# An input projection in two panels of seven products, with the row transposes moved between modulation steps

## The chip, the cores and the metric

The kernel runs on one core of a Trainium2 chip. The metric is the device time of one execution in microseconds (us). The work is float32 throughout.

## The reference, cut to what matters

The program computes three layers of a network. Only the start of the first one is touched: 512 latent rows `x` and 256 context rows `ctx` of width 1024 are normalised, modulated and multiplied by `w_in` (1024 x 2080).

```python
mod_x = (silu(c) @ w_ada + b_ada)            # 6 vectors of 1024: sh1, sc1, g1, sh2, sc2, g2
mod_c = silu(c_ctx) @ w_ada + b_ada
p_x = modulate(rmsnorm(h, norm_mix_w), sh1, sc1) @ w_in
p_c = modulate(rmsnorm(hc, norm_mix_w), csh1, csc1) @ w_in
# columns of p: q 256, k 256, v 512, g 512, r_f 16, r_b 16, pool_in 512
gk = log_sigmoid(r @ w_gk + b_gk) / 16       # for both directions
```

Of the context rows only k, v and r are needed. Behind this stand a gated linear attention with pooling (the mixer), an output product, and a layer of 32 experts which adds rows into a scratch array in memory that has to be zero beforehand.

## The kernel before, in words

The first block of the program works in stages, and the order on every engine is written out by hand; engines wait for each other by semaphores. At the end of the block all engines meet before the next block (the mixer) begins.

Weights pass through `ring`, a ring of tiles of 1 MB. In this block it has 8 slots, 0 to 7 (`MIX_SLOTS`). SP issues the loads in the order of the list `stream.tiles`; the load of tile n goes into slot n mod 8 and waits until the tile that held the slot is released (`stream.load`, line 188). The counter of releases is in order: `release` puts one on a matmul, and `owe` leaves it to be paid by the next `settle` or `release`. The list begins with tiles 0 to 7, eight blocks of `w_ada` (shift and scale of the first norm), then four tiles of `w_in` for q, k and v, and then, twice, two tiles of `w_in` and eight of `w_ada`. A tile of `w_in` is cut into rows of 2 KB per partition, a tile of `w_ada` into rows of 4 KB, in two issues.

In order of time TensorE does this:

- Three transposes bring the small vectors into columns (line 856). They wait for all constants `cst` (952 KB) and the vectors.
- Eight modulation steps (`vector_step`, line 543): four matmuls with 32 stationary columns each, side by side in the array, on one tile of `w_ada`. Their result is copied by VectorE (line 797), turned (line 571) and becomes `mod1` and `amix`.
- 48 transposes of x and ctx (lines 867 and 871) into `hT`, channels on partitions. ScalarE (x) and VectorE (ctx) move them out of PSUM and apply scale and shift on the way.
- q and k of x and k of the context (`project`, line 402), then r (line 891), v with the four `gates` between (line 902), g with eight further modulation steps between, and the pool input with the last eight.

VectorE and ScalarE empty PSUM, and between that turn r into the decays: `zb`, a log-sigmoid in three passes, four scans (line 835), `dve_shift`, `act_power`, `dve_scale`. GpSimd loads x and ctx, and when `mod_ready` is 3 it issues one DMA that fills the 20 MB of `y_scratch` with zeros (line 733); it waits for that DMA inside the block.

`Panel` and `Sums` are used by later layers. They compute a product of 512 x 1024 by 1024 x 1024 from four blocks of the weights and four of the rows with seven products of half the size in every direction instead of eight (Winograd's form). VectorE makes the sums of the weights t3, t2, t4, t1 in place, one after another, and the sums of the rows s1 to s4. Three pairs of the seven products add up in the same PSUM banks. A product is 16 matmuls of 256 columns (`channel_product`, line 459) or 8 of 512 (`token_product`, line 447).

## Time and profile before

| | us |
|---|---|
| median of 3 runs | 2180.89 |
| range of the 3 runs | 2178.28 to 2184.44 |
| the profiled execution | 2184.99 |
| its span on the core | 2182.8 |
| first matmul of q and k | 47.97 |
| first transpose of the mixer | 208.89 |

The span begins with the first instruction on the core; the 2.2 us between it and the time of the execution lie around it. Times inside are counted from the start of the span. An engine's busy time is the time in which it had an instruction in work; DMA queue q1 is the one that SP and ScalarE issue to in hardware, q0 is GpSimd's.

### The profile page before, as it was taken

How to read it: one execution, taken by the hardware profiler on the slowest of the kernel's cores; microseconds unless marked ns; L12 is line 12 of the kernel's file. 1: busy time of each engine (PE TensorE's matmuls, PEld its weight loads, DVE VectorE, ACT ScalarE, POOL GpSimd, SP SyncE). 2: the span in 40 equal slices, each digit the busy share in tenths (PEclk: the TensorE clock that was granted, in tenths of full speed). 3: DMA queues.
4: the chain of work that ended last, by engine and by line, in shares of the span. 5: the costliest groups of instructions: out<-in, count | busy, mean ns of one | idle time of the engine just before them, and what ended most of it. 6: DMA issues, size and time to landing. Idle time of an engine off the chain costs nothing.

```text
span 2182.8 us, 35887 instructions
## 1 busy us (share of the span) xinstructions
PE 2114.5 (97%) x14889; PEld 1141.3 (52%) x14889; DVE 950.8 (44%) x1640; ACT 491.0 (22%) x876; POOL 216.2 (10%) x266
## 2 busy tenths in 40 slices
PE   5999899999999999999999999899999999999998
PEld 2434545344444544444354443588584448777643
DVE  1041625833223223322322344754577625597742
ACT  2030312111101101110110110311126102666560
POOL 1000001121121122112112232200000000000000
PEclk9999999999999999999999999999999999999999
DMA  9957137999999999999999999723121032212200
GB/s 378 351 193 258 61 119 315 422 415 400 409 410 407 414 413 409 416 413 415 411 416 413 410 420 419 292 78 109 39 101 54 1 105 79 97 58 97 97 20 38
DMA packets 111830, 565.88 MB, mean 259 GB/s; under 512 B 16933, under 2 KB 29010, under 8 KB 77938
## 3 DMA queue, kind: packets, MB, share of 16 engines
q1 hardware_dynamic: 88950, 512.93, 58.4%
q0 software_dynamic: 19584, 49.84, 6.4%
q10 hardware_dynamic: 3228, 2.17, 0.3%
q8 instruction: 47, 0.77, 0.1%
q14 instruction: 21, 0.17, 0.0%
HBM read 545.21 MB, written 37.62 MB: 267 GB/s over the span
## 4 chain that ended last, share of the span: by engine, by line
PE 80%; DVE 3%; DMA 3%; issue 1%; ACT 1%; ACTq 0%; SPq 0%; DVEq 0%; POOLq 0%
PE ps L2309 30%; PE ps L459 11%; PE ps L2279 11%; PE ps L3848 5%; PE ps L3747 4%; PE ps L2287 4%; PE ps L447 3%; PE ps L1533 2%; PE ps L3727 2%; PE ps L3279 1%; DMA ring<-in_w_gu 1%; PE ps L3270 1%; DMA ring<-in_odd_w_in 1%; PE ps L2899 1%; PE ps L2943 1%
## 5 line engine op out<-in xcount | busy, mean ns | idle before, releaser
L2309 PE MATMUL ps<-ring,xeT 128*32 128x512 f32 x6144 | 684.5, 593 | 3.0 <-issue 1.7
L2309 PEld LDWEIGHTS ps<-ring,xeT 128*32 128x32 f32 x6144 | 259.9, 110 | 392.4 <-issue 335.5
L2279 PE MATMUL ps<-ring,mT 128*32 128x512 f32 x2048 | 322.3, 592 | 0.0
L2287 PE MATMUL ps<-ring,mT 128*32 128x256 f32 x2048 | 264.1, 379 | 0.0
L2048 DVE TENSOR_TENSOR mT<-ps,spread_bias 128x768 f32<-128x768 f32 x32 | 30.6, 957 | 462.5 <-PE ps L2309 462.4
L1986 ACT ACTIVATE mT<-mT 128x768 f32<-128x768 f32 x32 | 27.0, 845 | 867.0 <-DVE mT L2048 838.4
L2287 PEld LDWEIGHTS ps<-ring,mT 128*32 128x32 f32 x2048 | 118.3, 110 | 96.7 <-issue 66.2
L459 PE MATMUL ps<-hT_late,ring 128*128 128x256 f32 x704 | 155.5, 379 | 1.1 <-issue 1.1
L2279 PEld LDWEIGHTS ps<-ring,mT 128*32 128x32 f32 x2048 | 122.9, 110 | 52.8 <-issue 9.2
L459 PEld LDWEIGHTS ps<-hT_late,ring 128*128 128x128 f32 x704 | 133.4, 190 | 22.2 <-issue 4.1
L3848 PE MATMUL ps<-ring,mT 128*128 128x512 f32 x256 | 110.4, 592 | 0.0
L1808 POOL DMA_INDIRECT xe<-xn_scratch,idx x93 | 96.6, 1038 | 30.6 <-issue 28.7
L1819 ACT ACTIVATE xeT<-xturned,modx 128x96 f32<-128x96 f32 x248 | 91.8, 453 | 9.7 <-PE ps L2309 9.7
L2075 DVE STREAM_TRANSPOSE mT<-mT 128x768 f32<-128x768 f32 x31 | 30.3, 978 | 142.0 <-PE ps L2287 141.9
L3848 PEld LDWEIGHTS ps<-ring,mT 128*128 128x128 f32 x256 | 48.6, 190 | 60.8 <-issue 60.7
L1839 POOL TENSOR_TENSOR mark<-cst 128x1 f32<-128x1 f32 x57 | 11.9, 210 | 686.9 <-DVE ysb L2087 643.8
L402 PE MATMUL ps<-ring,hT 128*128 128x512 f32 x160 | 71.7, 598 | 0.0
L402 PE MATMUL ps<-hT,ring 128*128 128x512 f32 (+1 forms) x160 | 64.5, 556 | 2.2 <-DVE vtok L840 1.5
L1533 PE MATMUL ps<-ring,mixT 128*128 128x512 f32 x128 | 56.7, 596 | 2.4 <-DMA ring<-in_w_out 1.2
L1922 POOL DMA_INDIRECT y_scratch<-ysb,y_idx x54 | 55.6, 1029 | 23.1 <-issue 23.1
L459 PE MATMUL ps<-mT,ring 128*128 128x256 f32 x256 | 56.6, 379 | 0.0
L3747 PE MATMUL ps<-ring,mT 128*128 128x512 f32 x128 | 55.3, 592 | 0.0
(497 smaller groups left out, 2467.6 us busy)
## 6 DMA issues: line engine op xcount, KB each, us to landing
ring<-in_w_gu SPq DMA_DIRECT2D x128, 2048.0 KB, 9.4
ring<-in_w_down SPq DMA_DIRECT2D x128, 1024.0 KB, 28.2
y_scratch<-zeros POOLq DMA_DIRECT2D x1, 20352.0 KB, 99.1
ring<-in_even_w_in SPq DMA_DIRECT2D x18, 1024.0 KB, 7.3
ring<-in_w_ada SPq DMA_DIRECT2D x32, 512.0 KB, 8.0
ring<-in_odd_w_in SPq DMA_DIRECT2D x16, 1024.0 KB, 6.7
ring<-in_w_ada SPq DMA_DIRECT2D x8, 1024.0 KB, 20.1
ring<-in_w_in SPq DMA_DIRECT2D x8, 1024.0 KB, 18.4
```

The source lines that it names most:

```text
L402: mm = nc.tensor.matmul(dst, left(k, w, kk), right(k, w, kk), start=first, stop=last)
L447: mm = nc.tensor.matmul(out, left[:, k, t * P:(t + 1) * P], w[:, k, :], start=fresh and k == 0 and (n == BANK or t == 0), stop=k == 3, ski ...
L459: mm = nc.tensor.matmul(out, w[:, k, c * P:(c + 1) * P], left[:, k, :], start=fresh and k == 0 and c % 2 == 0, stop=k == 3, skip_group_che ...
L1533: mm = nc.tensor.matmul(bank(j_out[t, h].bank), mixT[:, k, t * P:(t + 1) * P], tiles[k // 2][:, k % 2, h * BANK:(h + 1) * BANK], start=k = ...
L1808: nc.gpsimd.indirect_dma_start(xe[:, q * DQ:(q + 1) * DQ], None, quarter_rows, bass.IndirectOffsetOnAxis(ap=idx[:, q:q + 1], axis=0), boun ...
L1819: nc.scalar.activation(xeT[:, j, 0:CAP].rearrange("p (q s) -> p q s", q=3), xturned[:].rearrange("p (q j s) -> p j q s", q=3, j=KD)[:, j], ...
L1922: nc.gpsimd.indirect_dma_start(y_parts[n], bass.IndirectOffsetOnAxis(ap=y_idx[:, n:n + 1], axis=0), src, None, bounds_check=(2 + 2 * n) * ...
L2279: mm = nc.tensor.matmul(quad(b, 2 * q + n), acted(k, q, src), w[:, kk, n * BANK:(n + 1) * BANK], start=first, stop=last)
L2287: mm = nc.tensor.matmul(quad(b + 1, c, 256), acted(k, 2, src), w[:, kk, c * 256:(c + 1) * 256], start=first, stop=last)
L2309: mm = nc.tensor.matmul(quad(q, c), left(q), part_columns(w, c), start=start, stop=stop)
L3747: mm = nc.tensor.matmul(bank(b), left[:, k, t * P:(t + 1) * P], w[k // 4][:, k % 4, :], start=fresh and k == 0, stop=k == KD - 1, skip_gro ...
L3848: return nc.tensor.matmul(bank(j.bank), mT[:, k, t * P:(t + 1) * P], w[:, k % 2, h * BANK:(h + 1) * BANK], start=k == 0, stop=k == 2 * KD - 1)
```

## The change

x keeps four of the five projections' columns in two panels. Panel one is q, k (columns 0 to 511) and g (1024 to 1535), panel two is v (512 to 1023) and the pool input (1568 to 2079); each is done in seven products. The context's k and v stay plain products, and run between the first two products of a panel (`context_keys`, `context_values`). The list of tiles becomes: 8 `w_ada`; blocks 12, 11, 21, 22 of panel one (tiles 8 to 11); `w_ada` steps 0 to 5 (12 to 17); block 11 of panel two (18); step 6 (19); block 21 (20); step 7 (21); blocks 12 and 22 (22 and 23); the last eight `w_ada` (24 to 31).

The 32 transposes of x move between modulation steps 3 to 6, and ScalarE copies them out plain; scale and shift of x are applied later by VectorE in SBUF. The zero fill waits for panel one's first product instead of `mod_ready`, and the wait for its end moves into the next block. Of `cst` only the identity is loaded first, the rest behind the first eight tiles.

```diff
-        add_panel(w_in, KD, 4, 0, 512)
-        add_panel(w_in, KD, 4, 512, 1024)
...
-        for c0, firsts in ((1024, (2 * D, 5 * D)), (1568, (3 * D, 4 * D))):
...
+        EARLY_ORDER = ("12", "11", "21", "22")
+        WOVEN_ORDER = ("11", "21", "12", "22")
+        early_at = []
+
+        def add_early(b, sides):
+            k0, c = 4 * (b[0] == "2"), sides[b[1] == "2"]
+            early_at.append(len(stream.tiles))
+            add(ktiles(w_in, k0, 4, c, c + BANK), 4, BANK)
+
+        def add_ada(ks, firsts):
+            for k in ks:
                 stream.add(ada_pieces(k, *firsts), (2, D))
+
+        for b in EARLY_ORDER:
+            add_early(b, (0, 1024))
+        add_ada(range(6), (2 * D, 5 * D))
+        add_early("11", (512, 1568))
+        add_ada((6,), (2 * D, 5 * D))
+        add_early("21", (512, 1568))
+        add_ada((7,), (2 * D, 5 * D))
+        add_early("12", (512, 1568))
+        add_early("22", (512, 1568))
+        add_ada(range(KD), (3 * D, 4 * D))
         end_inputs = len(stream.tiles)
...
+        j_tr = [psum.job((2, 3, 0)[k % 3], "act") for k in range(KD)]
...
+        j_trc = [psum.job(b, "act") for b in (5, 6, 7)]
...
+        p1 = early_job(2, "act")
+        j_z = [(psum.job(b, "dve"), psum.job(b + 1, "dve")) for b in (0, 4, 0, 4)]
+        p2 = early_job(4, "dve")
+        j_kc = psum.job(6, "act")
+        p_qkg = Panel(p1, p2, *end_of_panel(), early_at[:4], EARLY_ORDER, {})
+        p1, p2 = early_job(2, "act"), early_job(4, "dve")
+        j_vc = early_job(6, "dve")
...
+        weights, sums_ready, context = signal("weights"), signal("sums_ready"), signal("context")
+        quarter = lambda ap: ap.rearrange("p (k n) -> p k n", k=4)
+        early = Sums(hT[:, 0:4, 0:HALF], hT[:, 4:KD, 0:HALF], hT[:, 4:KD, HALF:T], quarter(scratch[:, 6144:7168]),
+                     quarter(scratch[:, 7168:8192]), hT[:, 0:4, HALF:T], quarter(g2b[:]), {})
+        qk_part = {"11": (qT[:, :, 0:HALF], kT[:, :, 0:HALF]), "21": (qT[:, :, HALF:], kT[:, :, HALF:T])}
+        g_part = {"12": sgT[:, :, 0:HALF], "22": sgT[:, :, HALF:]}
+        v_part = {"11": vtok[:, 0:2, :], "21": vtok[:, 2:4, :]}
+        pool_part = {"12": ptok[:, 0:2, :], "22": ptok[:, 2:4, :]}
...
-                vec_loads.on(sp.dma_start(cst[:], A["cst"]), 16)
+                vec_loads.on(sp.dma_start(ident, A["cst"][:, C_ID:C_ID + P]), 16)
                 sp.wait_ge(zeroed.sem, 2)
                 load_vectors(sp, 1)
+                stream.load(sp, 1, MIX_SLOTS)
+                wgk_loads.on(sp.dma_start(cst[:, C_ID + P:], A["cst"][:, C_ID + P:]), 16)
                 stream.load(sp, end_inputs - 4, MIX_SLOTS)
...
-                pool.wait_ge(mod_ready.sem, 3)
-                rows_zeroed.on(pool.dma_start(
-                    y_dram.rearrange("r (h n) -> (r h) n", n=BANK).rearrange("(p a) n -> p a n", p=CAP),
-                    zeros[0:CAP, :].unsqueeze(1).to_broadcast([CAP, (E + XB) * D // BANK, BANK])), 16)
-                rows_zeroed.wait(pool)
+                rows = y_dram.rearrange("r (h n) -> (r h) n", n=BANK).rearrange("(p a) n -> p a n", p=CAP)
+                p_qkg.p1.filled(pool)
+                rows_zeroed.on(pool.dma_start(rows, zeros[0:CAP, :].unsqueeze(1).to_broadcast(
+                    [CAP, (E + XB) * D // BANK, BANK])), 16)
...
+                for k, j in enumerate(j_tr):
+                    act_out(act, j, hT[:, k, 0:T], bank(j.bank))
+                act.wait_ge(mod_ready.sem, 2)
+                for i, j in enumerate(j_trc):
                     j.filled(act)
-                    j.empty(nc.scalar.activation(hT[:, k, 0:T], bank(j.bank), ACT.Identity,
-                                                 bias=mod1[:, k, 0:1], scale=amix[:, k, 0:1]))
-                for i, j in enumerate(j_qk):
+                    for half in range(2):
+                        k = 2 * i + half
+                        ins = nc.scalar.activation(hT[:, k, T:], ps[:, j.bank, half * TC:(half + 1) * TC], ACT.Identity,
+                                                   bias=mod1[:, k, 1:2], scale=amix[:, k, 1:2])
...
+                queries_and_keys(p_qkg.p1, "11")
...
+                j_kc.filled(act)
+                j_kc.empty(nc.scalar.activation(kT[:, :, T:], bank(j_kc.bank).rearrange("p (b n) -> p b n", b=2), ACT.Copy))
+                queries_and_keys(p_qkg.p6, "21")
+                act_out(act, p_qkg.p7, g_part["22"], by_channel(p_qkg.p7))
...
+                act_out(act, p_qkg.p3, g_part["12"], by_channel(p_qkg.p3), ACT.Silu)
+                p_qkg.p5.emptied_for(act)
+                nc.scalar.activation(g_part["22"], g_part["22"], ACT.Silu)
+                act_out(act, p_vp.p1, v_part["11"], by_token(p_vp.p1))
+                act_out(act, p_vp.p6, v_part["21"], by_token(p_vp.p6))
+                act_out(act, p_vp.p7, pool_part["22"], by_token(p_vp.p7))
+                act_out(act, p_vp.p3, pool_part["12"], by_token(p_vp.p3))
...
-                mod_ready.on(nc.vector.memset(stat[:, 60:61], 0.0))
...
+                for k, j in enumerate(j_tr):
+                    j.emptied_for(dve)
+                    h_ready.on(nc.vector.tensor_scalar(hT[:, k, 0:T], hT[:, k, 0:T], amix[:, k, 0:1], mod1[:, k, 0:1],
+                                                       ALU.mult, ALU.add))
+                h_ready.wait(dve)
+                w = {b: arrived(dve, i) for b, i in zip(p_qkg.order, p_qkg.at)}
+                weights_t3(dve, p_qkg, w)
+                a21 = early.s3
+                early.ready["s1"] = sums_ready.on(nc.vector.tensor_tensor(early.s1, a21, early.a22, ALU.add))
                 j_r.filled(dve)
                 j_r.empty(nc.vector.tensor_copy(rT[:, 0:T], bank(j_r.bank, T)))
                 j_rc.filled(dve)
                 j_rc.empty(nc.vector.tensor_copy(rT[:, T:], bank(j_rc.bank, TC)))
+                sums_ready.wait(dve)
+                early.ready["s2"] = sums_ready.on(nc.vector.tensor_tensor(early.s2, early.s1, early.a11, ALU.subtract))
+                early.ready["s3"] = sums_ready.on(nc.vector.tensor_tensor(early.s3, early.a11, a21, ALU.subtract))
+                sums_ready.wait(dve)
+                early.ready["s4"] = sums_ready.on(nc.vector.tensor_tensor(early.s4, early.a12, early.s2, ALU.subtract))
                 for i, (d, m) in enumerate(DM):
                     bias = vcol(("b_gk_f", "b_gk_b")[d], m)
                     for j, cols in zip(j_z[i], (slice(0, T), slice(T, W3))):
...
+                dve.wait_ge(context.sem, 1)
+                weights_t2(dve, p_qkg, w)
...
+                join_queries_and_keys(p_qkg.p2, p_qkg.p1, "11")
+                j_kc.filled(dve)
+                weights_t4(dve, p_qkg, w)
...
+                weights_t1(dve, p_qkg, w)
...
+                join_22(dve, p_qkg, g_part["22"], by_channel(p_qkg.p5))
+                join_queries_and_keys(p_qkg.p4, p_qkg.p6, "21")
+                p_qkg.p4.emptied_for(dve)
+                j_kc.emptied_for(dve)
...
+                w = {b: arrived(dve, i) for b, i in zip(p_vp.order, p_vp.at)}
+                weights_t3(dve, p_vp, w)
+                dve.wait_ge(context.sem, 2)
+                weights_t2(dve, p_vp, w)
+                join_11(dve, p_vp, v_part["11"], by_token(p_vp.p2))
+                j_vc.filled(dve)
+                j_vc.empty(nc.vector.tensor_copy(vtok[:, NT:, :], by_token(j_vc)))
                 j_gates.filled(dve)
                 j_gates.empty(nc.vector.tensor_copy(gate_rows, bank(j_gates.bank)))
+                weights_t4(dve, p_vp, w)
+                weights_t1(dve, p_vp, w)
+                join_22(dve, p_vp, pool_part["22"], by_token(p_vp.p5))
+                join_21(dve, p_vp, v_part["21"], by_token(p_vp.p4))
                 j_rows2.filled(dve)
...
-                vector_tiles(pe, j_rows)
...
+                for k in range(KD):
+                    mm = vector_step(pe, j_rows, k, take(pe)[:, 0, :])
+                    if k < KD - 1:
+                        stream.release(mm)
+                    else:
+                        stream.owe()
+                        j_rows.done(mm)
+                    if 3 <= k < KD - 1:
+                        if k == 3:
+                            pe.wait_ge(xn_ready.sem, NT)
+                        turn_x(2 * k - 6)
+                        turn_x(2 * k - 5)
+                pe.wait_ge(xn_ready.sem, NT + NTC)
+                for i in range(3):
+                    turn_context(i)
                 turn_vector_rows(pe, j_rows, j_mod[0], mod_rows)
...
+                turn_context(3)
...
+                        if j is j_r:
+                            pe.wait_ge(h_ready.sem, NT + NTC + 1 + k)
+                        elif k % 2 == 0:
+                            j_trc[k // 2].emptied_for(pe)
...
-                project(pe, 2, [(j, bank(j.bank), lambda k, w, kk, t=t: hT[:, k, tokens(t)],
-                                 lambda k, w, kk: w[:, kk, :]) for t, j in enumerate(j_v + j_vc)],
-                        before={k: lambda k=k: gates(k - 1) for k in range(1, 5)})
...
+                def rest_of_panel(p, product, b, done_with_p7, done_with_p5, done_with_p4):
+                    pe.wait_ge(weights.sem, p.ready["t2"])
+                    pe.wait_ge(sums_ready.sem, early.ready["s2"])
+                    product(pe, p.p6, early.s2, b["11"], False)
+                    pe.wait_ge(sums_ready.sem, early.ready["s3"])
+                    product(pe, p.p7, early.s3, b["12"], True)
+                    done(done_with_p7)
+                    pe.wait_ge(weights.sem, p.ready["t1"])
+                    product(pe, p.p5, early.s1, b["11"], False, True)
+                    done(done_with_p5)
+                    product(pe, p.p4, early.a22, b["21"], False, True)
+                    done(done_with_p4)
+                    pe.wait_ge(sums_ready.sem, early.ready["s4"])
+                    product(pe, p.p3, early.s4, b["22"], False, True)
+                    stream.owe()
+
+                def done(tiles):
+                    for _ in range(tiles):
+                        stream.owe()
+
+                def modulation_step(job, k):
+                    return vector_step(pe, job, k, take(pe).rearrange("p c n -> p (c n)"))
+
+                b = {"12": take(pe), "11": take(pe)}
+                channel_product(pe, p_qkg.p1, early.a11, b["11"], True, True)
+                context_keys(0, b["11"])
+                for i in range(4):
+                    gates(i)
+                b["21"] = take(pe)
+                channel_product(pe, p_qkg.p2, early.a12, b["21"], True)
+                context_keys(1, b["21"])
+                b["22"] = take(pe)
+                rest_of_panel(p_qkg, channel_product, b, 1, 1, 1)
+                for k in range(6):
+                    stream.release(modulation_step(j_gates, k))
+                b = {"11": take(pe)}
+                token_product(pe, p_vp.p1, early.a11, b["11"], True)
+                context_values(0, b["11"])
+                modulation_step(j_gates, 6)
+                b["21"] = take(pe)
+                token_product(pe, p_vp.p2, early.a12, b["21"], True)
+                context_values(1, b["21"])
+                j_gates.done(modulation_step(j_gates, 7))
+                b["12"], b["22"] = take(pe), take(pe)
+                rest_of_panel(p_vp, token_product, b, 0, 2, 3)
+                for k in range(KD):
+                    mm = modulation_step(j_rows2, k)
+                    if k < KD - 1:
+                        stream.release(mm)
+                stream.owe()
+                j_rows2.done(mm)
...
                     amat_zero.on(nc.gpsimd.memset(a, 0.0))
+                rows_zeroed.wait(pool)
```

The functions that the new code calls, `channel_product`, `token_product`, `weights_t1` to `weights_t4`, `join_11`, `join_21`, `join_22` and `act_out`, are those of lines 440 to 531 and stay as they are.

## Rows read from the trace of the kernel before

**Rows 1.** The page: busy engines over the span (share of it), with instructions.

```profile
PE 2114.5 (97%) x14889; PEld 1141.3 (52%) x14889; DVE 950.8 (44%) x1640; ACT 491.0 (22%) x876; POOL 216.2 (10%) x266
```

**Rows 2.** Windows of core 0: stretch, busy us (x instructions), granted clock, DMA share, GB/s.

```profile
246.00:248.00 2.00, 0.13 (x4) 0.00 (x0) 1.82 (x6) 1.97 (x4) 0.00 (x0) 1.00 0.00 0
248.00:252.00 4.00, 3.79 (x17) 3.57 (x18) 1.09 (x4) 0.06 (x1) 0.00 (x0) 0.58 0.02 4
```

**Rows 3.** Timeline of TensorE, 12 to 212 us: start, duration, engine, line, operands.

```profile
36.28 1.93 PE L543 MATMUL ps<-ring,scol 128*32 128x512 f32 x8 [0.73 <-DMA ring<-in_w_ada]
...
47.97 34.64 PE L402 MATMUL ps<-hT,ring 128*128 128x512 f32 x96 [0.71 <-ACT hT L763]
82.55 2.79 PE L891 MATMUL ps<-hT,wr 128*32 128x512 f32 x32
...
90.52 1.45 PE L902 MATMUL ps<-rT,wgk 128*128 128x512 f32 x4
91.81 5.31 PE L402 MATMUL ps<-ring,hT 128*128 128x512 f32 x12
...
171.60 3.70 PE L402 MATMUL ps<-ring,hT 128*128 128x512 f32 x8
175.23 1.06 PE L543 MATMUL ps<-ring,scol 128*32 128x512 f32 x8
176.22 3.70 PE L402 MATMUL ps<-ring,hT 128*128 128x512 f32 x8
...
208.89 0.85 PE L1141 MATMUL ps<-cst,ring 128*128 128x128 f32 x6 [1.20 <-PEq L713]
```

**Rows 4.** Timeline of TensorE in a later layer, products of two panels.

```profile
1555.99 7.03 PE L447 MATMUL ps<-ring,g2b 128*128 128x512 f32 x16
1562.86 7.03 PE L447 MATMUL ps<-ring,sgT 128*128 128x512 f32 x16
...
1604.18 7.07 PE L459 MATMUL ps<-g2b,ring 128*128 128x256 f32 x32
```

**Rows 5.** Timeline of VectorE, 0 to 208 us.

```profile
32.65 2.74 DVE L794 TENSOR_SCALAR res<-res,stat 128x1024 f32<-128x1024 f32 x4
...
40.41 0.25 DVE L805 SCALAR_TENSOR_TENSOR amix<-mod,vec 128x8 f32<-128x8 f32 x2
...
91.58 1.14 DVE L823 TENSOR_SCALAR ring<-ps,vec 128x512 f32<-128x512 f32 x2 [5.75 <-PE ps L902]
...
126.49 6.70 DVE L835 TENSOR_TENSOR_SCAN res<-cst,ring 128x768 f32<-128x768 f32 x4
```

**Rows 6.** Groups of instructions of VectorE over the whole span.

```profile
L496 DVE TENSOR_TENSOR ring<-ring 128x2048 f32<-128x2048 f32 x7 | 16.0, 2289 | 10.9 <-issue 8.3 <-PE ps L459 2.5
```

**Rows 7.** DMA queues, 48 to 141 us: packets, MB, share of 16 engines.

```profile
q0 software_dynamic: 5104, 20.84, 67.6%
q1 hardware_dynamic: 2401, 7.58, 21.3%
```

**Rows 8.** The same queues, 50 to 66 us.

```profile
q0 software_dynamic: 857, 3.51, 57.1%
q1 hardware_dynamic: 827, 2.96, 45.3%
```

**Rows 9.** DMA issues of the span: queue, KB each, median us to landing.

```profile
y_scratch<-zeros POOLq DMA_DIRECT2D x1, 20352.0 KB, 99.1
```

**Rows 10.** Timeline of GpSimd, 40 to 50 us.

```profile
41.47 3.23 POOL L733 DMA_DIRECT2D y_scratch<-zeros  x1 [37.42 <-DVE stat L809]
```

**Rows 11.** The tile ring on the SP queue, issues of 20 to 23 us.

```profile
L188 SPq DMA_DIRECT2D ring<-in_w_in x1: 1873/1873/1873, 21.1 to 21.1; - x1
...
DMA to landing us min/median/max: 20.7/20.7/20.7
```

**Rows 12.** The same tile, issues of 83 to 85 us.

```profile
L188 SPq DMA_DIRECT2D ring<-in_w_in x1: 379/379/379, 83.6 to 83.6; - x1
...
DMA to landing us min/median/max: 22.4/22.4/22.4
```

168 lines of the change are left out of this document (80 added, 88 removed).

## The prediction, on record before the result

> **What bounds the kernel now.** I read the page first: TensorE is busy in 97% of the span [rows 1], so what shortens TensorE's list shortens the kernel, unless something else then ends last. Next its timeline through the input stage [rows 3]. The last modulation step on the path starts at 36.28 us and takes 1.93; the projections start at 47.97; the next block's first transpose at 208.89 comes after 1.20 idle, so the stage's matmuls end at 207.69. Between 47.97 and 207.69 the rows follow each other with next to no gap: 159.7 us of matmuls, bound by TensorE alone. Third, the DMA queues. From 48 to 141 us they carry two things at once, 20.84 MB of zeros on q0 and 7.58 MB of weights on q1 [rows 7]. The fill is issued at 41.47 and lands 99.1 us later, at 140.6 [rows 9, 10]; as the view from 48 on holds all its bytes (20352 KB), its first packet comes some 6.5 us after its issue. TensorE doesn't wait for it now: most tiles are in the ring before it starts, and the others are requested long before their use. Whether that stays so decides this case.
>
> **What the change takes from TensorE.** A product by tokens is 6.87 us (1555.99 to 1562.86); one by channels lasts 7.07 in its row against 7.03, so 6.9 from start to start [rows 4]. A product by tokens is 8 matmuls of 512 columns, so one is 0.86 us. In plain form a panel is 64 of these, in seven products 56: 8 x 0.86 = 6.9 us less, 13.7 for two panels. The alternation of four projection matmuls with a modulation step costs 3.63 and 0.99 [rows 3]; four matmuls alone are 3.44, so sixteen such groups lose some 2.7 us more, which bare steps in a row don't. As a check on the 159.7: q and k 32 of these matmuls, the context's keys 8, v 32 and its context 16, g and pool 64, so 152 x 0.86 = 130.6, r 2.7, gates 5.2, sixteen steps 15.8, changes 2.7, together 157.0; the 2.7 left are small waits. Afterwards it is 136 matmuls, 117 us.
>
> **The front.** Transposes of x (32 of 48) go into the gaps in which TensorE waits for tiles of w_ada; the constants (0.91 MB of them) go behind w_ada. At the 6.47 MB in 16 us that the full queues move [rows 8], 0.404 MB/us, that brings the last step forward by 2.3 us, from 36.3 to 33.9, and its end to about 35. Then: VectorE's copy and the turn of the rows up to `amix`, 2.5 us as now (38.21 to 40.66 [rows 3, 5]; three context turns now stand in front of the rows' turn, mostly beside the copy), then eight scale-and-shift operations of 512 columns. The trace has the 1024-column one at 0.69 (2.74 for four [rows 5]), so 0.36 each, 2.9 together. r follows each of them closely and ends near 41.2. The first product needs tile 9. Its place in the byte order is the same as now, and tile 9 lands at 21.1 + 20.7 = 41.8 [rows 11]. So product one starts at 41.8. Now r ends 2.7 us (82.55 to 85.26) into its own slot behind q and k; counted alike, the front gives 47.97 + 2.7 - 41.8 = 8.9 us. Should the clock be at half there, some 1 to 2 us are lost; I take 1.
>
> **TensorE's list afterwards, if nothing waits for weights.** Product one to 48.7. Context keys, half, 3.4: 52.1. Four gates of 1.29 (90.52 to 91.81 [rows 3]): VectorE must first do t3 (2.29 [rows 6], from tile 11 at 47), s1 to s4 (1.2 each by the same rate) and the copies of r, so that the third and fourth gates and product two, which reuse banks, wait for evictions of 1.14 [rows 5]: 2 us of stall, 59.3. Product two 66.2, keys 69.6, p6 76.5, p7 83.4, p5 90.3, p4 97.2, p3 104.1. VectorE between: t2 by 61.6, t4 by 72, t1 78.9 (p6 must be over), scans 6.7 [rows 5] and shifts to 89, before p5 is over: no stall. Six bare steps 110; p1 117; context values 124; step 125; p2 132; values 138.6; step 139.6; five products 174; eight steps 182. That would be 25.7 us before 207.7, less 1 for the clock: 8.9 of the front, 13.7 of products, 2.7 of changes and the 2.7 of small waits, less the 2 of the new stall.
>
> **What the weights do.** Panel one holds its four slots until its products end. The releases are: tile 8 at the start of p5 (83.4), tile 9 at p4 (90.3), tile 10 at p3 (97.2), tile 11 and the steps' tiles from 105 on. So tiles 16, 17 and 18 are requested then, 19 to 23 at 105 to 108, and VectorE's t3 of panel two wants all four blocks, the last being tile 23. Products p6 and p7 stand behind t3 and t2. And the fill now begins at 48.7 + 6.5 = 55.2, when only tiles 15 and later are outstanding, runs alone until about 83, and is then beside exactly these tiles. How fast? While three or more tiles are queued behind each other, q1 moved 2.96 MB in 16 us beside 3.51 MB of zeros, 5.7 us a tile [rows 8]; a single w_in tile requested at 83.6 in the middle of the fill took 22.4 us [rows 12], where 2.6 are its bytes. The pace that includes all this is 28.4 MB in the 92.6 us from 48 to 140.6, 0.307 MB/us [rows 7, 9]. Up to tile 23 the queues must move, from 55.2 on, the fill and tiles 15 to 23: 20.84 + 9 x 1.05 = 30.3 MB, 98.6 us. Tile 23 lands at about 154. Lower end: tiles 16 to 23 at 5.7 us each from 91 (the 83.4 and some 8 us until a lone tile flows, an estimate between nothing and the 22.4): 137. Upper end: the lone w_in tile's pace again and again, 165 (worked out below).
>
> With 154: t3 and t2 4.6 us, 158.4, where the list above wanted p6 at 139.6: a wait of 19 us. On the way tile 18 is some 6 to 9 us late as well, which is part of the 19. After such a pause TensorE starts at half clock: after 1.9 us of idling in 246 to 248 the mean clock of the next four us was 0.58 [rows 2], which is 3.4 us at 1.2 GHz and 1.7 us lost; after a longer pause I take 2.5. Five products 34.4: 195.3; eight steps 7.9: 203.2. At the end of the block nothing else is late: the last tiles are requested from p4 on, when the fill is over. With the 1 us of the front: 204.2, that is 3.5 us before 207.7. Behind the block everything moves with it; the fill's end (about 155) is long before the mixer's GpSimd asks for it. The profiled execution would be 2185.0 - 3.5 = 2181.5; the median of the runs shown lies 4.1 below that execution, so 2177.4.
>
> The Trainium skill (DMA: Bandwidth & Descriptors, section "Queues, rings and completion order") says that each DMA engine takes turns between the queues that have work, packet by packet. By that a w_in tile alone beside the fill would take the time of its 1.05 MB and of 2.1 MB of zeros, 8 us, and the trace's 22.4 us disagrees; if the rule held for tiles 16 to 23, tile 23 would be there near 145. This is the second case below.
>
> **The rivals.**
> *The fill takes turns fairly.* Once eight tiles are queued one behind the other, they might all go at 5.7 to 7 us. For it speaks the queued pace [rows 8], against it the 22.4 us of a single tile [rows 12]; and tiles 16 to 18 are requested one at a time. Tile 23 lands between 137 and 150, the block ends at 185 to 200: 2158 to 2173, say 2168 (tile 23 at 145).
> *The fill starves the second panel.* Place: tiles 18, 20, 22, 23, all of w_in in short rows, each taking 22.4 us as the one in rows 12 did, the w_ada tiles 5.7 between: 97.2 + 22.4 = 119.6, then 125, 148 and 153 for tiles 19 to 21, and 176 for tile 22, unless the fill ends first. By the pace above it does, near 155 to 160, and then 22 and 23 take 2.6 us each: 165 at the latest. It decides from the point where tile 23 lands after 157.5, since all that was saved in front of it is then used up. With 165 the block ends at 215.2: 2188.4.
> *The DMA doesn't matter.* Tiles are there in time as now; the list gives 182 to 183, 2156. Against: the requests come 28 us and more after the fill's start, and 8.4 MB must pass within 50 us beside it.
>
> **How the numbers follow.** A difference of 0.3% (6.5 us) is about what a measurement of this kernel can tell from none. The likeliest case, tile 23 at 150 to 160, ends within it: 0.45, for 2177.4 with its own range 2172 to 2185. Fair turns 0.34 and no effect of the DMA 0.06 are faster: 0.40. Starving and mishaps that I don't see, 0.15, are slower. The range of 2163 to 2187 leaves out the no-wait case, the lower end of the fair one and the upper end of starving.
>
> **What would show it.** TensorE's timeline: product one starting near 42, products 6.9 apart, t1 done before p7 ends; a pause before the first product of panel two (tile 18) and a larger one before its p6, released by VectorE's t2, which itself waits for a DMA into `ring`. The fill's issue near 49 and its landing near 155. DMA share full from 83 to 150. The prediction is wrong if a single tile beside the fill lands in under 10 us, if the fill is over much before 150, or if VectorE, not a DMA, is what panel one waits for.

## The result and the profile after

The changed kernel took 2189.74 us (median of 5 runs, 2186.32 to 2191.97) against 2180.89 (5 runs, 2178.28 to 2184.44): a ratio of 1.0039, interval 1.0027 to 1.0052. It is slower, by 8.9 us; 2177.4 had been forecast, with 2163 to 2187 as the range. Its profiled execution has a span of 2188.5 us. One execution of the experiments (2878.4 us, granted clock 0.741, in the run with the second part of the fill behind panel two's first product) fell in a slower state and is left out; all the others ran at 0.984 or more.

The page's first part, TensorE now and the DMA share in 40 slices of 54.7 us:

```profile
PE 2098.8 (96%) x14969; PEld 1120.5 (51%) x14969; DVE 973.8 (44%) x1652; ACT 497.6 (23%) x887; POOL 217.1 (10%) x266
...
DMA  9974326999999999999999999723121022212200
```

TensorE is busy for 15.7 us less than in [rows 1], and the kernel is longer all the same: the work saved has come back as idle time. The timeline of TensorE through the stage shows where (start, duration, operation; in brackets the idle time before it and what ended it):

```profile
39.53 5.01 PE L979 MATMUL ps<-hT,wr 128*32 128x512 f32 x32 [0.80 <-DVE hT L853]
44.48 7.17 PE L475 MATMUL ps<-hT,ring 128*128 128x256 f32 x32
...
58.09 2.82 PE L990 MATMUL ps<-rT,wgk 128*128 128x512 f32 x8 [0.41 <-DVE ring L873]
61.81 7.14 PE L475 MATMUL ps<-hT,ring 128*128 128x256 f32 x32 [0.90 <-DVE ring L873]
...
99.87 7.07 PE L475 MATMUL ps<-g2b,ring 128*128 128x256 f32 x32
...
112.67 1.07 PE L559 MATMUL ps<-ring,scol 128*32 128x512 f32 x8 [1.30 <-DMA ring<-in_w_ada]
126.40 8.63 PE L463 MATMUL ps<-ring,hT 128*128 128x512 f32 x16 [12.66 <-DMA ring<-in_w_in]
...
143.04 7.13 PE L463 MATMUL ps<-ring,hT 128*128 128x512 f32 x16 [0.15 <-DMA ring<-in_w_in]
...
169.59 9.20 PE L463 MATMUL ps<-ring 128*128 128x512 f32 x16 [11.56 <-issue]
178.63 7.03 PE L463 MATMUL ps<-ring,hT 128*128 128x512 f32 x16
...
214.35 1.57 PE L559 MATMUL ps<-ring,scol 128*32 128x512 f32 x8 [1.95 <-DMA ring<-in_w_ada]
217.13 1.08 PE L1297 MATMUL ps<-cst,ring 128*128 128x128 f32 x4 [1.22 <-PEq L737]
```

Panel one runs as a chain of 7 us products with 1.3 us of waits (0.41 and 0.90). Panel two stands still twice, before its first product (for tile 18, a `w_in` tile) and before its sixth. The mixer's first transpose comes at 217.13 where it came at 208.89 [rows 3], 8.2 us later. What released the sixth product is in VectorE's timeline (t3, then t2, which ends at 169.4):

```profile
164.66 2.29 DVE L506 TENSOR_TENSOR ring<-ring 128x2048 f32<-128x2048 f32 x1 [57.84 <-DMA ring<-in_w_in]
167.09 2.29 DVE L512 TENSOR_TENSOR ring<-ring 128x2048 f32<-128x2048 f32 x1
```

So the last tile of panel two, tile 23, landed at 164.6, and t3 and t2 followed it without a gap. Behind the stage the difference still grows, to 12.0 us at the w_out product (285.43 against 273.45): the mixer takes 68.3 us where it took 64.6, with granted clocks of 0.72 in its first 8 us and 0.58 from 257 to 269, against 1.00 and 0.87 at the same steps before. The fill in the page's list of DMA issues (queue, KB, us from issue to landing):

```profile
y_scratch<-zeros POOLq DMA_DIRECT2D x1, 20352.0 KB, 113.7
```

GpSimd issues it at 52.3, so it lands at 166, after 113.7 us against 99.1 [rows 9]. Next the two queues in four windows of the changed kernel, 58 to 84, 104 to 119, 119 to 145 and 145 to 166 us (packets, MB, share of 16 engines):

```profile
q0 software_dynamic: 1946, 7.97, 100.0%
...
q0 software_dynamic: 807, 3.31, 68.1%
q1 hardware_dynamic: 770, 2.02, 33.7%
...
q0 software_dynamic: 1022, 4.15, 45.7%
q1 hardware_dynamic: 1664, 3.95, 39.1%
...
q1 hardware_dynamic: 923, 2.74, 37.3%
q0 software_dynamic: 203, 0.80, 12.3%
```

Alone, the fill moves 7.97 MB in 26 us, 0.31 MB/us. Beside the tiles the packets go one for one (807 and 770), and as a packet of zeros is 4.1 KB and the tiles' mean one 2.6 KB, the weights get 38% of the bytes. In the last window the engines are half idle (37.3 and 12.3%) while TensorE waits for tile 23, and from 160 to 166 us they are busy for 10.7 and 3.8%, as much as two or three of the 16 would be by themselves (an estimate from the share). The other engines are through: the fill ends on them at very different times, and the tile lands when the slowest has moved its part.

SyncE's issues of tiles 22 and 23 are late as well. First the changed kernel, then the same issues in the run of the next section's first experiment, with no zeros in this stage (start, duration of the two together):

```profile
119.96 16.51 SPq L188 DMA_DIRECT2D ring<-in_w_in  x2
...
110.39 1.33 SPq L188 DMA_DIRECT2D ring<-in_w_in  x2
```

In the changed kernel tile 23's issue begins at 122.2 and lasts 14.3 us, in which SyncE waits for no release of a slot. So zeros in the queues hold up not only the packets of a tile but also the issuing of those behind it. What the issue waits for isn't in the trace.

A further loss in the stage is the clock: the granted clock of 115 to 130 and of 159 to 174 us, the stretches with the two pauses, is 0.54 of full speed, so part of each at the 1.2 GHz level. The two products behind the pauses take 8.63 and 9.20 us instead of 7.03.

```profile
115.00:130.00 15.00, 3.60 (x5) 1.71 (x6) 0.00 (x0) 0.00 (x0) 0.00 (x0) 0.54 0.98 354
159.00:174.00 15.00, 4.41 (x6) 1.94 (x7) 9.20 (x6) 0.00 (x0) 0.00 (x0) 0.54 0.09 36
```

### The profile page after: what moved, and what is told of

It reads as the page before. It is cut to its first block, busy times and chain, and to the rows that moved or that the text cites. A ratio compares the mean times of both kernels' runs of the same rounds, so it can differ in the third digit from the quotient of the medians.

```text
span 2188.5 us, 36130 instructions
## 1 busy us (share of the span) xinstructions
PE 2098.8 (96%) x14969; PEld 1120.5 (51%) x14969; DVE 973.8 (44%) x1652; ACT 497.6 (23%) x887; POOL 217.1 (10%) x266
## 4 chain that ended last, share of the span: by engine, by line
PE 79%; DVE 3%; DMA 3%; issue 1%; ACT 1%; ACTq 0%; POOL 0%; SPq 0%; POOLq 0%; DVEq 0%
PE ps L2465 30%; PE ps L475 11%; PE ps L2435 10%; PE ps L4004 5%; PE ps L2443 5%; PE ps L3903 4%; PE ps L463 3%; PE ps L1689 2%; PE ps L3883 2%; DMA ring<-in_w_gu 1%; PE ps L3435 1%; PE ps L3426 1%; DMA ring<-in_odd_w_in 1%; PE ps L3055 1%; PE ps L3099 1%
## 5 line engine op out<-in xcount | busy, mean ns | idle before, releaser
L2465 PE MATMUL ps<-ring,xeT 128*32 128x512 f32 x6144 | 677.5, 593 | 3.7 <-DMA ring<-in_w_gu 2.5
L2465 PEld LDWEIGHTS ps<-ring,xeT 128*32 128x32 f32 x6144 | 234.7, 110 | 412.0 <-issue 400.3
L2435 PE MATMUL ps<-ring,mT 128*32 128x512 f32 x2048 | 308.0, 592 | 0.7 <-DMA ring<-in_w_down 0.7
L2443 PE MATMUL ps<-ring,mT 128*32 128x256 f32 x2048 | 228.4, 379 | 0.0
L2443 PEld LDWEIGHTS ps<-ring,mT 128*32 128x32 f32 x2048 | 99.2, 110 | 109.9 <-issue 105.9
L2435 PEld LDWEIGHTS ps<-ring,mT 128*32 128x32 f32 x2048 | 106.0, 110 | 54.8 <-issue 15.5
L506 DVE TENSOR_TENSOR ring<-ring 128x2048 f32<-128x2048 f32 (+1 forms) x10 | 21.8, 2180 | 104.8 <-DMA ring<-in_w_in 64.7
L475 PEld LDWEIGHTS ps<-mT,ring 128*128 128x128 f32 x256 | 48.6, 190 | 6.6
## 6 DMA issues: line engine op xcount, KB each, us to landing
y_scratch<-zeros POOLq DMA_DIRECT2D x1, 20352.0 KB, 113.7
```

Of the source, the lines that this page charges most:

```text
L475: mm = nc.tensor.matmul(out, w[:, k, c * P:(c + 1) * P], left[:, k, :], start=fresh and k == 0 and c % 2 == 0, stop=k == 3, skip_group_che ...
L2435: mm = nc.tensor.matmul(quad(b, 2 * q + n), acted(k, q, src), w[:, kk, n * BANK:(n + 1) * BANK], start=first, stop=last)
L2443: mm = nc.tensor.matmul(quad(b + 1, c, 256), acted(k, 2, src), w[:, kk, c * 256:(c + 1) * 256], start=first, stop=last)
L2465: mm = nc.tensor.matmul(quad(q, c), left(q), part_columns(w, c), start=start, stop=stop)
```

## The experiments

Each row compares with the kernel before on the same chip. Chips differ (its medians there were 2187.31 for the first four, 2186.73 for the next four, 2170.39 for the four after and 2181.02 for the last two), so ratios are to be compared, not times. "Mixer" is the start of its first transpose in the profiled execution, "t3" that of panel two's t3, which follows tile 23's landing at once.

| run | us | ratio, interval | t3 | mixer |
|---|---|---|---|---|
| fill whole in the mixer | 2203.25 | 1.0078 [1.0059, 1.0097] | 125.3 | 186.1 |
| fill 40 rows + 66 in the mixer | 2168.57 | 0.9921 [0.9904, 0.9937] | 125.5 | 186.0 |
| fill whole, at the second `mod_ready` | 2182.26 | 0.9977 [0.9967, 0.9987] | 150.7 | 201.3 |
| before, fill 39 us later | 2204.69 | 1.0078 [1.0061, 1.0095] | - | 226.5 |
| changed kernel again | 2197.58 | 1.0047 [1.0032, 1.0062] | 163.7 | 215.3 |
| before, fill 40 + 66 in the mixer | 2189.89 | 1.0010 [1.0001, 1.0018] | - | 209.8 |
| fill 40 + 66 at panel two's p6 | 2204.79 | 1.0082 [1.0067, 1.0097] | 125.5 | 221.7 |
| fill in rows of 1 KB | 2174.65 | 0.9939 [0.9921, 0.9957] | 143.6 | 194.9 |
| neighbouring rows apart in memory | 2177.99 | 1.0039 [1.0026, 1.0052] | 162.9 | 214.3 |
| fill in two halves | 2166.37 | 0.9982 [0.9973, 0.9991] | 149.4 | 200.8 |
| fill 40 + 66 at panel two's p1 | 2161.90 | 0.9958 [0.9945, 0.9971] | 125.3 | 197.1 |
| the same, constants first | 2163.19 | 0.9963 [0.9950, 0.9975] | 126.8 | 198.6 |
| fill 40 + 26 + 40 | 2161.70 | 0.9911 [0.9897, 0.9924] | 125.5 | 185.9 |
| fill 40 + 66 in the mixer again | 2160.62 | 0.9909 [0.9896, 0.9923] | 125.5 | 189.0 |

**Theory.** The change is worth some 20 us and the fill takes them back, since every tile requested beside it comes late. **Rival.** Panel one holds its four slots until its products end, so that panel two's tiles are requested too late whatever the queues carry; then moving the fill gives nothing.

### The fill moved out of the stage

```
@@ GpSimd, block of the projections @@
...
-                p_qkg.p1.filled(pool)
-                rows_zeroed.on(pool.dma_start(rows, zeros[0:CAP, :].unsqueeze(1).to_broadcast(
-                    [CAP, (E + XB) * D // BANK, BANK])), 16)
@@ GpSimd, block of the mixer @@
...
-                rows_zeroed.wait(pool)
+                pool.wait_ge(row_loads.sem, 32)
+                rows_zeroed.on(pool.dma_start(rows, zeros[0:CAP, :].unsqueeze(1).to_broadcast(
+                    [CAP, (E + XB) * D // BANK, BANK])), 16)
@@ GpSimd, end of the block that stores xn2 @@
                 xn2_stored.wait(pool)
+                rows_zeroed.wait(pool)
```

> The changed kernel with the whole zero fill moved out of the input stage: GpSimd issues it at the start of the mixer, behind the two row loads, and waits for it at the end of the block after the mixer. Theory (the fill stands beside panel two's tiles): the two pauses of 12.7 and 11.6 us before panel two's first product and before its p6 vanish, tile 23 lands near 118, the stage's matmuls end at 184 to 188 instead of 215.9, and the median falls to 2160 to 2170, depending on what the fill costs beside the mixer's own loads. Rival (VectorE's sums or TensorE's longer list set the end of the stage): the stage still ends after 205 and the median stays above 2180.

Every pause in the stage is gone: t3 at 125.3 instead of 164.7, panel two's first and sixth product without a wait, the mixer at 186.1. But the mixer block ends with the fill: issued at 193.8, it lands 94.9 us later, at 288.7, and the next block's first product, w_out, starts at 289.2. The program's own wait for the fill stands only at the end of that next block, so the block's end itself waited for GpSimd's transfer; two runs with the fill in two parts show the same (landings at 253.9 and 221.1, the next block at 254.2 and 221.5). The time, 2203.25, is far from the 2160 to 2170 that I expected. TensorE's timeline of that run:

```profile
183.78 1.07 PE L559 MATMUL ps<-ring,scol 128*32 128x512 f32 x8 [1.15 <-DMA ring<-in_w_ada]
186.08 1.51 PE L1296 MATMUL ps<-cst,ring 128*128 128x128 f32 x6 [1.23 <-PEq L737]
...
289.23 6.09 PE L1689 MATMUL ps<-ring,mixT 128*128 128x512 f32 x7 [36.37 <-PEq L1114]
```

The rival falls: with the same releases of slots, but no zeros, no tile of panel two is late. The fill costs the changed kernel 31 us in the stage (217.1 - 186.1), and this one 36.4 at the mixer's end.

### The fill cut in two: 40 of 106 rows behind product one, 66 in the mixer

```
@@ against the run above: GpSimd, block of the projections @@
+                p_qkg.p1.filled(pool)
+                rows_zeroed.on(pool.dma_start(rows[:, 0:40], zeros[0:CAP, :].unsqueeze(1).to_broadcast([CAP, 40, BANK])), 16)
@@ GpSimd, block of the mixer @@
-                rows_zeroed.on(pool.dma_start(rows, ...
+                rows_zeroed.on(pool.dma_start(rows[:, 40:], ...
```

> The changed kernel with the fill in two parts: 40 of its 106 rows per partition behind panel one's first product (they can pass in the 26 us in which no tile is outstanding), the other 66 at the start of the mixer. Theory: nothing of the fill is beside tiles 17 to 23, the stage ends at 184 to 189, and the smaller rest disturbs the mixer's loads less than the whole one: 2158 to 2166, at or below the variant with the whole fill in the mixer. Rival (any fill before the panel's tiles costs its own length, as the queues are conserved): the stage ends 8 or more us later than in that variant.

0.9921, the mixer at 186.0; at 2168.57 us it lies just above the 2158 to 2166 expected. TensorE's timeline of that run:

```profile
183.71 1.06 PE L559 MATMUL ps<-ring,scol 128*32 128x512 f32 x8 [0.81 <-DMA ring<-in_w_ada]
186.01 0.85 PE L1299 MATMUL ps<-cst,ring 128*128 128x128 f32 x6 [1.23 <-PEq L737]
...
254.44 22.55 PE L1692 MATMUL ps<-ring,mixT 128*128 128x512 f32 x48 [3.23 <-PEq L1117]
```

The 40 rows (7.9 MB) are over on the slowest engine by 89.5, when of the stage's later tiles only one, of `w_ada`, has been requested (from 86.8 on). The 66 land 59.9 us after their issue and end as the mixer does, with 3.23 us of wait at the w_out product instead of 36.37.

### The fill earlier

```
-                p_qkg.p1.filled(pool)
+                pool.wait_ge(mod_ready.sem, 2)
```

> The changed kernel with the fill's wait put back to the modulation vectors (mod_ready), as in the kernel before: it is issued at about 39 instead of 52. Theory (pace of the queues from the fill's start to tile 23): everything behind is up to 13 us earlier, less some us because tiles 9 to 15 share the queues and product one starts later: tile 23 at 153 to 158, stage end 204 to 210, 2178 to 2184. Rival (what counts is only that tiles 16 to 23 are requested one at a time beside a fill): as slow as the changed kernel, 2187 or more.

Issued at 39.3, 13 us earlier. t3 comes 14.0 us sooner (150.7), the pause before panel two's first product falls to 7.64 and the one before its sixth vanishes, the mixer starts at 201.3. Against that r ends, and product one starts, 3.4 us later (47.88), as part of r waits for VectorE (42.87 [2.09 <-DVE hT]), whose eight scale-and-shift operations take 6.41 us instead of 3.74; product two starts 4.9 us later. The balance is 0.9977, as the theory had it: the earlier the fill, the less of it is left when panel two's tiles are requested. What slows VectorE beside the start of the fill is left open.

### The kernel before, with the fill later

```
-                pool.wait_ge(mod_ready.sem, 3)
+                j_qk[0].filled(pool)
```

> The kernel before with its fill put off until q's first bank is done (79 instead of 41.5 us), with its own order of projections. Theory: lateness alone costs the old order little, since its tiles are requested 20 us and more before use; tiles 17, 18 and 19 land late without effect, and those requested at 152 to 157 in a row take up to 7 us each, needed from 170 on: 2181 to 2188. Rival (a late fill costs its overlap in any order): 2190 or more.

The kernel before loses as well once its fill goes out at 80.5 instead of 41.5, 1.0078: three of its woven modulation steps wait 5.27, 0.89 and 6.44 us, and the matmuls behind the two long waits lose 4.2 more at the 1.2 GHz level. I had expected 2181 to 2188; the rival's 2190 or more holds. So it isn't the products' form that makes a kernel sensitive to the fill, but which tiles are requested beside it.

### The changed kernel again, and the kernel before with the split fill

```
@@ the kernel before: GpSimd, where the fill was; the wait moves to the block that stores xn2 @@
...
-                rows_zeroed.wait(pool)
+                rows_zeroed.on(pool.dma_start(rows[:, 0:40], ...
@@ GpSimd, block of the mixer @@
+                pool.wait_ge(row_loads.sem, 32)
+                rows_zeroed.on(pool.dma_start(rows[:, 40:106], ...
```

> The changed kernel once more, beside the three below on one chip, as their reference. If its loss is its own and not its chip's: 1.003 to 1.005 of the kernel before, the pauses before panel two's first product and before its sixth at 12 and 11.5 us again. If the loss came from one chip: 0.998 to 1.002.

> The kernel before with the fill in two parts: 40 of 106 rows at the old place, 66 in the mixer behind its two row loads, waited for where the rows of y are first needed. Theory (the change itself is worth some 20 us and only the fill hides it; TensorE before waits for no tile): 0.999 to 1.003, so that nothing of the 0.992 that the changed kernel reached with this fill is the fill's own. Rival (the whole fill already costs the kernel before some time, by bank or queue contention that stretches its matmuls): 0.996 or less.

On another chip the changed kernel gives 1.0047, with pauses of 12.33 and 11.18 us at the same two products. The kernel before doesn't gain from the split (1.0010). So with the same fill the change itself is worth 0.9921 / 1.0010 = 0.991, 19 us, and as it stands it loses 9. (The two ratios are from two chips; at the mixer's start the difference is 23.8 us, 209.8 against 186.0, so some 4 of it are gone by the end.) The two executions also answer what becomes of the loss behind the stage. TensorE's timeline of the changed kernel, at its router product and at the last long group of matmuls:

```profile
364.69 4.01 PE L2404 MATMUL ps<-mT,res 128*128 128x96 f32 x32
...
2120.37 4.88 PE L4004 MATMUL ps<-ring,mT 128*128 128x512 f32 x11
```

and of the kernel before with the split fill:

```profile
355.28 4.01 PE L2250 MATMUL ps<-mT,res 128*128 128x96 f32 x32
...
2110.98 14.32 PE L3850 MATMUL ps<-ring,mT 128*128 128x512 f32 x33
```

9.41 us apart at the first place and 9.39 at the second: in this pair nothing is given back. (In the first pair of traces the 11.7 us at the router, 364.66 against 352.94, shrink to 5.7 at the end; the profiled execution of the kernel before lay 4.1 us above its median, which accounts for 4.1 of the 6.)

### The second part at panel two's sixth product, or at its first

```
@@ GpSimd, block of the projections: 40 rows behind p_qkg.p1, then @@
+                p_vp.p6.filled(pool)          # in the other run: p_vp.p1.filled(pool)
+                rows_zeroed.on(pool.dma_start(rows[:, 40:106], ...
```

> The changed kernel with 40 rows behind panel one's first product and 66 behind panel two's sixth, from about 130 us on, where the queues stood empty until 180 when they were put into the mixer. Theory: no tile of panel two is late, the w_out product no longer waits the 3.2 us, 0.989 to 0.992 of the kernel before, the mixer starting at 186 to 187. Rival (any fill beside single tiles delays them by 20 us and more: the modulation tiles requested from panel two's fifth product on are late too): waits of 5 to 12 us in the last eight steps, 0.995 or more.

> The changed kernel with 40 rows behind panel one's first product and 66 behind panel two's first (about 119 us): their packets should run from 126 to 162, after the last tile of panel two has landed (125) and before the last modulation tiles are requested (from 163 on). Theory (only tiles that are requested while zeros are in the queues are slow): no pause over 1 us in the stage, the mixer starts near 186, no wait of 3 us at the w_out product, 0.989 to 0.992 of the kernel before. Rival (the second part meets the tiles in any case, as it did when issued at 149): 0.997 or more, waits among the last eight steps.

Both theories were too hopeful. I had taken p6 to end at 130; it ends at 149, so the zeros run from 155 to 221 straight through the requests of the last modulation tiles, and the last steps wait 26.6 us together. The block's end then waits for the fill too:

```profile
221.70 1.51 PE L1298 MATMUL ps<-cst,ring 128*128 128x128 f32 x6 [5.85 <-PEq L737]
```

That is 5.85 where it is 1.23 without zeros; with 4.4 us for five steps at the 1.2 GHz level this makes up nearly all of the 35.7 by which the mixer starts later than at 186.0, and the ratio is 1.0082. Issued at 119.5 instead, the part lands 64.4 us later, at 183.9, and the last steps still wait 6.8 us, with the steps behind the waits at the 1.2 GHz level (1.94 us instead of 1.07); 0.9958. Here I had reckoned with the pace of all queues together. The queue window of 134 to 150 us, where the fill is alone, shows

```profile
q0 software_dynamic: 1216, 4.98, 100.5%
q1 hardware_dynamic: 3, 0.01, 0.1%
```

that is 0.31 MB/us at a full share, 42 us for 13.0 MB on the mean engine and some 16 more on the slowest. The same kind of window of the run with the part at p6, 173 to 182 us, shows `w_ada` tiles (4 KB packets) beside the fill:

```profile
q0 software_dynamic: 405, 1.66, 61.5%
q1 hardware_dynamic: 404, 1.47, 40.1%
```

Packets again one for one, and with packets of one size nearly equal bytes: here as there the engines alternate, whatever the size.

### Shorter packets of zeros, or a split fill

```
-    rows = y_dram....rearrange("(p a) n -> p a n", p=CAP)
+    rows = y_dram....rearrange("(a p) n -> p a n", p=CAP)      # neighbouring rows apart

-    rows ... n=BANK ... one transfer
+    rows ... n=BANK // 2 ... two transfers of 106 rows of 1 KB each

+    rows[:, 0:53] behind p_qkg.p1, rows[:, 53:106] behind p_qkg.p3      # halves
```

> The changed kernel with the same bytes of zeros in rows of 1 KB instead of 2 KB (two transfers, as one holds too many rows). If the engines take turns packet by packet, a packet of zeros is half as long, a single tile beside the fill waits half as long, tiles 16 to 18 land in 10 to 15 us rather than 26, the pause before panel two's first product falls below 5 us. If the lone tile is slow because what was queued before it goes first, it stays at 20 us or more, and if shorter rows also move fewer bytes per us, tile 23 lands later than 164 and the time is 2190 or more (ratio 1.005 to 1.02). I take the second.

> The changed kernel with the same single fill at the same place, but with neighbouring rows of zeros 96 rows apart in memory, so that two 2 KB rows can't travel as one packet of 4 KB. Theory (the engines take turns packet by packet; a w_in packet of 2 KB stood against one of 4 KB of zeros, so a w_in tile had a third of the bytes and a w_ada tile half): packets of zeros of 2 KB, shares of a half and two thirds, tile 18 by about 113 and tile 23 by 132 to 140, the fill over at 160 to 170, the pause before panel two's first product under 3 us, before its sixth under 3 us, 0.990 to 0.996 of the kernel before. Rival (what was queued first goes first, packets don't matter): tile 23 at 160 and later, 1.003 or more. If 2 KB packets move fewer bytes per us, the fill's end runs into the last eight steps and 2 to 6 us of waits come back there.

> The changed kernel with the fill in two halves of 53 rows each of 2 KB, the second behind panel one's last product (about 107 us), close to where the second transfer of the run with 1 KB rows went out (111 us). If that run gained by its split and not by its short rows, this one gives the same: the second half's first packet at 114, tile 23 at 140 to 148, a pause of 3 to 8 us before panel two's sixth product, 0.993 to 0.997 of the kernel before. If the short rows did it: 1.000 or more, tile 23 at 155 or later.

The rows of 1 KB gave 0.9939, against my expectation, and for a reason that neither theory named. GpSimd's timeline of that run:

```profile
52.45 3.28 POOL L761 DMA_DIRECT2D y_scratch<-zeros  x1 [48.42 <-PE ps L475]
111.38 3.25 POOL L761 DMA_DIRECT2D y_scratch<-zeros  x1 [55.65 <-issue]
```

The second transfer, though next in GpSimd's list, went out only at 111.4, when the first had landed (58.5 us after its issue). So it is a fill in two halves, and between them few zeros are in the way (470 packets of them from 100 to 125 us, 1282 in the changed kernel), and panel two's first tiles come through. Its packets were no shorter, 7.54 MB in 1840 from 58 to 84 us, 4.1 KB each. Nor did rows that are apart in memory shorten them: in the queue window of 104 to 119 us of that run

```profile
q0 software_dynamic: 813, 3.33, 68.6%
q1 hardware_dynamic: 777, 2.01, 33.6%
```

4.1 KB (4096 bytes) again, the pauses 10.56 and 11.45, the ratio 1.0039. Whether shorter packets of zeros would help stays open, since neither edit made any. The fill in two halves of 2 KB rows, the second issued at 107.1, has no wait before panel two's first product and 12.38 us before its sixth; 0.9982. So part of the gain comes from the split, as expected, but it isn't the same as that of the 1 KB rows: those had 6.29 us there, their second half starting 4 us later and t3 coming 5.8 us earlier. Its range (0.993 to 0.997) was missed. What the other 4 parts in a thousand are, the runs don't settle; one difference on record is that SyncE had issued tiles 22 and 23 by 113.0 in the run with 1 KB rows, before its second half's packets, and only by 117.7 in the other.

### The constants in one piece

```
-                vec_loads.on(sp.dma_start(ident, A["cst"][:, C_ID:C_ID + P]), 16)
+                vec_loads.on(sp.dma_start(cst[:], A["cst"]), 16)
```

with the later piece's load gone, and the fill as in the run at p1.

> The kernel of the run above with the whole table of constants loaded first again, as before, instead of its first part first and the rest behind the first tile. By the prediction's step these 0.9 MB cost 2.3 us of the front: modulation steps, the rows' turn and the first product 2.0 to 2.5 us later, 0.0009 to 0.0012 more than the run above. Rival (the front is bound by the order of the later loads, not by these bytes): within 0.5 us.

The last early modulation step starts at 37.32 instead of 34.84 and r at 41.52 instead of 39.04: 2.5 us of the front, as the prediction's step has it (2.3). At panel one's second product (63.15 against 61.68) and at the mixer 1.5 are left, for VectorE's t3, behind which that product stands, waits for tile 11 and starts only 0.6 us later (49.86 against 49.27). The ratios, 0.9963 and 0.9958, can't be told apart.

### Three parts

40 rows behind product one, 26 behind panel two's first, 40 in the mixer.

> The changed kernel with 40 rows behind panel one's first product, 26 behind panel two's first (about 119 us; from 126 on, 5.1 MB, at 0.31 MB/us some 17 us, on the slowest engine some 25: over by 151, before the request at 163) and 40 in the mixer. Theory (zeros harm only what is requested before the slowest engine has finished them): no pause in the last eight steps beyond the 0.8 of the two-part kernel, the mixer starts within 0.5 us of 186, a shorter mixer part ends near 235, so up to 2 us less than the two-part kernel run beside it, 0.990 to 0.992 of the kernel before. Rival (zeros there cost time whenever they run): waits among the last steps, 0.994 or more, slower than the two-part kernel.

> The kernel with 40 rows behind panel one's first product and 66 in the mixer again, on the chip of the run above: 0.991 to 0.993 of the kernel before as in its first run. If that run was its chip's own: 0.995 or more.

The middle part is issued at 119.4 and lands 25.8 us later, at 145.2, before the next request, and the last steps wait 1.07 us in all: here a part between the requests did no harm, its slowest engine being done in time. The w_out product comes at 252.4 after 1.18 us, the value that it had before the change too. Against two parts (2161.70 and 2160.62 us) no gain can be told: both are at 0.991 of the kernel before. (The two-part kernel's profiled execution waited 3.03 us in its last step this time, 0.81 the first time.)

## Why the prediction was wrong

**Right: what TensorE saves.** The list without waits was to end at 182. In the run with the fill away it ends at 184.9 (186.1 less the 1.2 of the block's change), with products 6.9 apart. Of the difference 2.0 is the front (product one at 43.8 in this run) and 1.15 a wait before the last step.

**Mis-sized: the front.** Product one starts at 44.5, not 41.8. VectorE's eight scale-and-shift operations take 3.74 us, 0.47 each against the 0.36 that I had halved from one of 1024 columns, and r, whose first half follows them, takes 5.0 us and ends at 44.5; tile 9 isn't what product one waits for. The fill moves with it: issued at 52.3, it has its first packets at 57.2, not 55.2. The bytes of the constants were worth 2.5 us (2.3 forecast).

**Failed: "Tile 23 lands at about 154".** It landed at 164.6, 10.6 us late, and this alone carries the kernel across the point that the second rival names (157.5): the mixer was to start at 205.4 (204.2 and the 1.2 of the block's change) and starts at 217.1, and 10.6 of these 11.7 us are tile 23. The step took one mean pace, 0.307 MB/us, for the fill and tiles 15 to 23. With all their engines busy the queues do move 0.31 MB/us of zeros alone and 0.36 beside the tiles; but from 119 on the engines are through with the fill one after the other, and in the last 21 us before its end only 3.5 MB move, 0.17 MB/us. A mean pace says when the mean engine is done, a tile waits for the slowest.

Of the 10.6 us 2 are the fill's later start. Tile 15, which the sum counts, had all but landed by then, which takes some 3 off. Against that 2 MB of tiles 24 and 25 passed before tile 23 was there, 6.5 us at the forecast's pace: they were issued behind it, and I had them requested from p4 on. The other 5 are a mean pace of 0.293 instead of 0.307, which had the fill's tail of the kernel before already in it. I put the 2 MB and the pace down to the uneven engines; no run separates them from the late issues, for the same step had tiles 19 to 23 requested by 108, and tile 23's issue lasted from 122.2 to 136.5.

The second rival said 165 for tile 23 and 2188.4 us; 164.6 and 2189.7 were measured. That its number fits is in part luck: it had the fill over at 155 to 160 and two tiles of 2.6 us behind it, where the fill ended at 166 and tile 23 landed before that.

**Its mechanism was only half right.** The rival has tiles at 22.4 us each, one after the other. What runs show is two things. Engines alternate packet by packet, as the packet counts already say in [rows 8] (857 and 827), of which I had read only the bytes; the Trainium skill (DMA: Bandwidth & Descriptors, section "Queues, rings and completion order") has this rule, and the prediction wrongly held the 22.4 us of [rows 12] against it. That tile's time, in the queue windows of the kernel before of 88 to 97 and 97 to 106 us:

```profile
q0 software_dynamic: 550, 2.25, 78.9%
q1 hardware_dynamic: 386, 0.77, 22.0%
...
q0 software_dynamic: 717, 2.94, 94.9%
q1 hardware_dynamic: 132, 0.26, 7.4%
```

Requested at 83.6, it has three quarters of its packets between 88 and 97 (386, beside 550 of zeros), and the last quarter takes nine more, at 7.4% of the engines' time. So this lone tile cost some 4 us until it flowed, 9 of turns, and a tail of 9. Tile 18 of the changed kernel, requested at 100.5, landed 25.9 us later; I had it 6 to 9 us late, and TensorE stood 12.66 us before it.

**The other terms.** The pauses of panel two, 12.66 and 11.56 us, with 1.6 and 2.2 for the clock at the 1.2 GHz level (I had put 2.5 on one), and the smaller waits of 1.95, 1.30 and 0.15, make 31.4 us, against the 31.1 by which removing the fill brings the mixer forward (that run keeps 1.15 us of waiting and has its front 0.65 earlier). Of these I had 19 + 2.5. The 1.95 was forecast as nothing; 1.15 of it is there without any zeros. That behind the block everything moves with it wasn't so either: the mixer itself took 3.7 us more. The stall of panel one, 2 us in the forecast, is 1.3. The "fair turns" rival had the turns right and the range wrong (137 to 150): it lacked the tail.

## What to carry to other kernels

A transfer without a deadline isn't free while the tiles next to it have one: place it by when the tiles beside it are requested, and size each part so that its slowest queue engine, not the mean one, is done before the next request and before the block ends. Where two queues share the engines, read packets as well as bytes; and ask of every saving on TensorE which slots it holds longer, as that moves the requests. A work-saving change that came out 9 us slower was worth 19 us once 66 of the 106 rows of zeros were issued elsewhere.

## What was not expected of the hardware

- A software-queue transfer of zeros from rows of 2 KB and of 1 KB went in packets of 4.1 KB both times (7.97 MB in 1946 packets, 7.54 in 1840), with destination rows adjacent or 96 apart.
- Its end differs between engines by far: a part of 7.9 MB, issued at 52.3, moves 2.33 MB from 70 to 77 us, 1.16 from 77 to 83 and 0.26 from 83 to 90, with its landing at 89.4. In this last stretch its share is 13.6%, as much as 2.2 of the 16 engines would take (an estimate from the share). The Trainium skill (DMA: Bandwidth & Descriptors, section "Latency and other measured facts") says that two of the 16 engines are usually slower, with the software queue's descriptor rings as a guess at the cause. That agrees in number; which engines they are the views don't show.
- The second of two transfers of 10176 rows of 1 KB went out only after the first had landed (58.5 us after its issue), though nothing in the program held it back.
- An issue of SyncE, 0.4 us long where the queues are free, lasted 14.3 us beside the fill (tile 23, from 122.2).
- A block's end came 0.3 to 0.5 us after the landing of a transfer of GpSimd's for which the program waits only a block later (288.7 and 289.0, 253.9 and 254.2, 221.1 and 221.5).
